# Third channel tile of a causal depthwise convolution moved from TensorE to ScalarE products and GpSimd sums

## The reference, cut to what matters

```python
h = val * sigmoid(gate)                                  # (1, 512 positions, 512 channels)
h = conv1d_depthwise_causal(h, cv_w, width=31) + cv_b    # out[c, s] = sum_n cv_w[n, c] * h[c, s - 30 + n] + cv_b[c]
h = silu(layer_norm(h, cv_ln_g, cv_ln_b))
```

## Time and profile before

| what | us |
|---|---|
| median of three executions | 2161.75 |
| the profiled execution's own time | 2158.83 |
| its span, first to last instruction | 2157.0 |
| `s5_and_conv`, start of its first to start of the next part's first work | 112.4 to 177.4 |
| mean granted PE clock, whole span | 0.976 of full |

### The profile page before, as it was taken

One profiled execution on the slowest core, in us unless ns is written; L12 is line 12 of the kernel. 1 busy time (PEld: TensorE's weight loads), 2 busy tenths in 40 slices (PEclk: granted clock), 3 DMA queues, 4 the chain that ended last, 5 costly groups with the idle time before them and its releaser, 6 DMA issues. The chain is left out here.

```text
span 2157.0 us, 26506 instructions
## 1 busy us (share of the span) xinstructions
PE 2008.3 (93%) x8626; PEld 1004.3 (47%) x8626; DVE 757.6 (35%) x2018; ACT 401.4 (19%) x880; POOL 263.5 (12%) x253
## 2 busy tenths in 40 slices
PE   8998989999999999977998888998999999999976
PEld 4553554444444444433457555554444444444432
DVE  4692352222222222234111778443222222222216
ACT  2103021111111111100001555211111111111110
POOL 0001100111111111100210000300111111111110
PEclk9999999999999999988998999999999999999998
DMA  7133156999999999879002000216899999999957
GB/s 228 8 62 144 66 220 245 396 417 405 410 397 405 405 395 391 345 293 271 0 0 79 1 1 2 94 49 253 317 407 399 417 408 407 398 413 401 402 222 324
DMA packets 107424, 566.06 MB, mean 262 GB/s; under 512 B 38624, under 2 KB 39392, under 8 KB 69088
## 3 DMA queue, kind: packets, MB, share of 16 engines
q1 hardware_dynamic: 79136, 498.06, 58.2%
q0 software_dynamic: 28224, 67.16, 7.9%
HBM read 539.84 MB, written 59.77 MB: 278 GB/s over the span
## 5 line engine op out<-in xcount | busy, mean ns | idle before, releaser
L438 PE MATMUL moe_bank<-moe_weights,moe_xgT 128*128 128x512 f32 x1024 | 457.0, 599 | 16.7 <-DMA moe_weights<-in_ex_weights 16.3
L438 PEld LDWEIGHTS moe_bank<-moe_weights,moe_xgT 128*128 128x128 f32 x1024 | 189.9, 190 | 233.5 <-issue 215.9
L746 DVE TENSOR_TENSOR moe_hid<-moe_sil,moe_bank 128x256 f32<-128x256 f32 x98 | 41.3, 422 | 659.1 <-ACT moe_sil L621 659.1
L471 PE MATMUL moe_bank<-moe_weights,moe_hidT 128*128 128x512 f32 x512 | 230.5, 593 | 0.0
L441 PE MATMUL moe_bank<-wide,moe_xgT 128*64 128x512 f32 x512 | 226.6, 595 | 0.0
L441 PE MATMUL moe_bank<-moe_weights,moe_xgT 128*64 128x512 f32 x512 | 226.6, 595 | 0.0
L314 POOL DMA_INDIRECT y<-moe_xy,moe_rows x98 | 98.9, 1009 | 945.7 <-DVE moe_idx L726 559.3
L621 ACT ACTIVATE moe_sil<-moe_bank 128x256 f32<-128x256 f32 x98 | 37.6, 383 | 658.6 <-PE moe_bank L438 457.2
L754 DVE TENSOR_SCALAR moe_xy<-moe_bank,moe_sgate 128x512 f32<-128x512 f32 x98 | 73.6, 751 | 219.5 <-PE moe_bank L471 142.1
L471 PEld LDWEIGHTS moe_bank<-moe_weights,moe_hidT 128*128 128x128 f32 x512 | 92.4, 191 | 93.4 <-issue 93.4
L299 POOL DMA_INDIRECT moe_xy<-h,moe_idx x98 | 100.2, 1022 | 267.9 <-DVE moe_idx L726 240.4
(11 more groups left out here) (354 smaller groups left out, 2416.3 us busy)
## 6 DMA issues: line engine op xcount, KB each, us to landing
moe_weights<-in_ex_weights SPq DMA_DIRECT2D x96, 2048.0 KB, 20.7
moe_weights<-in_ex_weights SPq DMA_DIRECT2D x96, 1024.0 KB, 17.9
wide<-in_ex_weights SPq DMA_DIRECT2D x34, 2048.0 KB, 22.4
wide<-in_ex_weights SPq DMA_DIRECT2D x34, 1024.0 KB
moe_weights<-y SPq DMA_DIRECT2D x18, 1024.0 KB, 20.6
wide<-y SPq DMA_DIRECT2D x8, 1024.0 KB, 7.8
moe_xy<-y SPq DMA_DIRECT2D x6, 1024.0 KB, 26.8
oddin_win<-in_od_w_in_heads SPq DMA_DIRECT2D x1, 4288.0 KB, 19.1
```

Of the source, the lines that this page charges most:

```text
L438: mm = pe.matmul(bG[:, :], xgT[:, n, :], wgu[j][:, :, n, :], start=(n == 0), stop=(n == KC - 1))
L471: mm = pe.matmul(bY[half][:, :], hidT[:, n, :], wdn[j][:, n, cols], start=(n == 0), stop=(n == HC - 1))
```

## The change

PLAIN becomes 2, so PAIRED becomes 2: PE keeps tiles 0 and 1, tile 3 stays on DVE as it was, and tile 2 becomes plain. ACT computes the 31 tap products of tile 2, the first two straight into the even and the odd sum, the other 29 into a ring of six buffers in `wide`. POOL adds product n into the sum of its parity, and at last the two sums into one. ACT's product n waits until POOL has made the sum that frees its buffer; POOL's sum n waits for the product and for the previous sum of the same parity. ACT issues products 0 to 18 ahead of its first copy, 19 to 24 between the copies of the two halves, and 25 to 30 after them. The shifted input of tile 2 is written by one DVE instruction instead of four, DVE makes no diagonals for it, and `wide` is filled to its last column (4096 + 2 x 512 + 6 x 512 = 8192).

```diff
-TAPS, CT, PLAIN = 31, 4, 1
+TAPS, CT, PLAIN, RING = 31, 4, 2, 6
 PAIRED = CT - PLAIN
...
-        odd_sums = wide_flat[:, PAIRED * 2 * NPAIR * HP:PAIRED * 2 * NPAIR * HP + PLAIN * SEQ].rearrange("p (t s) -> p t s", t=PLAIN)
+        spare = wide_flat[:, PAIRED * 2 * NPAIR * HP:].rearrange("p (t s) -> p t s", s=SEQ)
+        odd_sums, ring = spare[:, 0:PLAIN], spare[:, PLAIN:PLAIN + RING]
...
-        taps_v = s.sem("taps_dve")
+        taps_v, products_a, sums_p = s.sem("taps_dve"), s.sem("products_act"), s.sem("sums_pool")
...
             pool.memset(toep[:], 0.0).then_inc(cleared, 1)
             pool.memset(state[:, :, :, 0], 0.0).then_inc(padded, 1)
+            sums = [yT[:, CT + PAIRED, :], odd_sums[:, 0, :]]
+            for n in range(2, TAPS):
+                pool.wait_ge(products_a, n + 1)
+                if n >= 4:
+                    pool.wait_ge(sums_p, n - 3)
+                pool.tensor_tensor(sums[n % 2], sums[n % 2], ring[:, n % RING], ALU.add).then_inc(sums_p, 1)
+            pool.wait_ge(sums_p, TAPS - 2)
+            pool.tensor_tensor(sums[0], sums[0], sums[1], ALU.add).then_inc(sums_p, 1)
...
         def _(act):
+            def products(a, b):
+                for n in range(a, b):
+                    shifted, tap = e.h2[0][:, PAIRED, n:n + SEQ], plain_taps[:, 0, n:n + 1]
+                    if n == 0:
+                        act.activation(yT[:, CT + PAIRED, :], shifted, ACT.Identity, scale=tap, bias=col["cv_b"][:, PAIRED:PAIRED + 1]).then_inc(products_a, 1)
+                    elif n == 1:
+                        act.activation(odd_sums[:, 0, :], shifted, ACT.Copy, scale=tap).then_inc(products_a, 1)
+                    else:
+                        if n >= 2 + RING:
+                            act.wait_ge(sums_p, n - 1 - RING)
+                        act.activation(ring[:, n % RING], shifted, ACT.Copy, scale=tap).then_inc(products_a, 1)
+
+            products(0, 19)
             for b in range(4):
                 h, q = b // 2, b % 2
+                if b == 2:
+                    products(19, 25)
                 act.wait_ge(y_done, h + 1)
...
+            products(25, TAPS)
             for t in range(1, PAIRED):
                 act.wait_ge(conv_done, t + 1)
```

## The result

The changed kernel takes 2170.82 us (median of 8 runs, 2169.14 to 2171.64), the kernel before 2161.77 us in 8 runs beside them. The ratio is 1.0042, 95% interval [1.0029, 1.0055]: slower by 9 us, just under the 0.5% that the prediction had named as its bound. The prediction was 2172 us. The profiled execution took 2171.09 us, against a sum of 2170.4 made for such an execution; its span is 2169.3 us, 12.3 more than before.

A forecast was written before the change was run, and what follows sets the result against it. PE, with DVE close behind, bounds the part before the change; after it DVE would end last, at 187.2. 2158.8 + 10.6 for the part + 1.0 for the clock = 2170.4 us profiled, given as 2172; range 2147 to 2184.

The forecast's parts named there:

- PE and DVE relieved: Tile 2 off PE saves 13.85 us, its diagonals off DVE 2.3; PE would end at 162.0, DVE at 160.4.
- ACT: 31 products of 128x512 beside everything, 0.55 us apiece, costing nothing by their length.
- POOL's rate: 30 adds of 128x512 at 1.26 us, 37.8 us in all; POOL undisturbed would end at 154.4.
- The turns: POOL's adds and DVE's instructions alternate, 1.68 us per pair; DVE ends 26.8 us later, at 187.2.
- the lock: A two-SBUF-input DVE instruction and a POOL instruction reading SBUF exclude each other; the second waits for the first.
- (a): Rival, chance 0.18: wide instructions hardly block each other; the part ends with PE at 162.8, 2145 to 2148 us.
- the last seven adds: POOL's adds during DVE's plain sum, predicted to start at about 164 and end at about 176.
- (c): Rival, chance 0.15: DVE goes first wherever it queues without a gap, POOL last; +16.6 us and clock, 2177 to 2179.
- price per add: What each paid POOL add costs DVE: 1.03 us taken, bounded by nothing and 1.26 us.
- The clock: PE's slow clock at the next part's start, after some 9 us idle: between 0 and 2 us, 1 taken.
- The sum: Whole kernel: 2158.8 + 10.6 + 1.0 = 2170.4 us for the profiled execution; 2172 given.
- (b): Rival, chance 0.12: the engines share, an add costing DVE about 0.5 us; about 2157 us, no change told.

The follow-up runs named there:

- experiment 1: Changed kernel with POOL's 30 adds replaced by memsets of a 128x960 scratch tile, tile 2's sum left out; 2181.3 us, with one round of the experts more.
- experiment 5: Changed kernel with ACT issuing products 25 to 30 together with 19 to 24, ahead of the copies of half 1; 2169.27 us (1.0037).
- Experiment 2: Changed kernel with each multiply-add of DVE's plain sum waiting for the one just before it; 2169.82 us (1.0047).
- 3: Changed kernel with the 29 multiply-adds of DVE's plain sum made adds, tile 3's taps left out; 2163.15 us, one execution, other experts chosen.
- experiment 8: Changed kernel with POOL's adds gated as in experiment 6, but DVE's two sums of tile 3 left in SBUF; 2170.28 us (1.0052).
- experiment 6: Changed kernel with DVE's tile 3 sums in PSUM and POOL's adds kept out of the rotations, 26 after half 1's state; 2154.24 us (0.9972).

## Why the prediction was right

**PE and DVE relieved.** Right. Without collisions (experiment 1) the part ended with PE and ACT's copy, the next one starting at 164.49; the prediction had the copy end at 162.8 and 0.8 us to the next part, 163.6.

**ACT.** Right that its 31 products cost nothing, though each took 0.61 to 0.72 us and not 0.55. Product 18 and the copies behind it never waited for POOL in a way that mattered: the copies of half 0 came at 142.9, behind PE. It was POOL that waited: products 19 to 24 stand behind these copies, and POOL ran dry for 1.31 us, up to 145.25, while one of DVE's scans ran in its old 1.19 us.

**POOL's rate.** 1.26 us, as read from the odd mixer. Its first add took 1.58, behind DVE's copy of the decays.

**The turns.** The deciding step, and right for the rotations: 1.68 us for an add and a DVE instruction was predicted; POOL's adds there stand 1.67 to 1.68 us apart beside the multiplies and adds. The state of half 1 was ready at 156.1, predicted 156.9. Here the row seen with small instructions and the Trainium skill's rule ("SBUF — State Buffer", section "Who interferes with whom") gave the right answer for wide ones, which no row that the prediction shows had. The rule's half on writes bears out too: memsets left the two-operand instructions alone (0.68 us in experiment 1). They held up the copy, which the Trainium skill counts in the same section among the instructions that can take the shared ports.

One reading was missed. Against the lock the prediction counts that "no row shows a wide DVE instruction waiting". The trace of before has one, the copy of the decays behind the memset of `toep` (experiment 1). It is of another kind than the rotation's, but it takes away that point for (a).

**Where it failed.** The step "I take it that the two engines take turns when both have something queued" does not hold for the last seven adds: POOL had run out of products at 155.6, came back at 165.15 in the middle of DVE's unbroken chain and got in only at its end. DVE ended at 180.2 instead of 187.2 and POOL at 187.57 instead of 176: rival (c) for that stretch. It moved the sum little, since either way one of the two is always at work. In turns an add costs 1.02 us more, alone behind the chain 1.22, which for the last five adds makes about 1 us (an estimate); in experiment 5, with turns throughout, the part is 1.05 us shorter, counted from its first matmul. That the end came out at 187.57 on POOL for a predicted 187.2 on DVE is in this stretch luck: the price per add was right, the order was not. Experiment 2 shows that a gap opens the door, 3 that the kind of instruction doesn't matter, 5 and 8 that POOL keeps its turns in the same gapless chain if its adds run on into it. Why a fresh add stands in this chain and gets in between the diagonals (experiment 6) stays open.

**The clock.** The term of +1 us was near nothing in the next part. The windows view of the changed kernel:

```profile
148.00:156.00 8.00, 0.00 (x0) 0.00 (x0) 7.90 (x5) 0.23 (x1) 7.55 (x5) 0.50 0.30 85
156.00:168.00 12.00, 11.75 (x76) 8.41 (x78) 11.97 (x19) 4.62 (x8) 2.85 (x1) 0.50 0.13 23
...
182.00:192.00 10.00, 3.54 (x5) 1.58 (x6) 2.74 (x5) 3.57 (x4) 5.49 (x5) 0.51 0.23 69
```

After both idle times of PE, 9.68 and 8.92 us long, the granted clock was 0.50, that is 1.2 GHz: `across(1)` took 7.09 us instead of 3.79, tile 1's convolution 16.26 instead of 13.96, the mean 5.35 instead of 3.67. The first two hid behind POOL, the last behind the transfer for which the following matmuls wait: from the mean to the first matmul of the experts it is 28.79 us, before 28.80. So the term measured nothing. The prediction also had PE idle for about 12 us ahead of `across(1)`; it was 9.68, in part because tile 0's convolution took 15.65 us instead of 13.96, with a granted clock of 0.50 from 121 to 123 us behind an idle time of 3.12. In experiments 3 and 5 the same convolution took 13.96 behind the same idle time, so this differs from execution to execution.

**The sum.** +10.6 for the part was predicted, 11.05 measured. The median moved by 9.05 us, the profiled execution by 12.3; the part's own shift lies between them and within the interval of the ratio (6.3 to 11.9 us). That the sum of 2170.4 comes within 0.7 us of 2171.09 is more than it can claim: single executions of the kernel before range from 2155.85 to 2166.2. What it had right is the price of a turn.

**The rivals.** (a) needs what experiment 1 had to create, a POOL that reads nothing. (b) is out: an add cost 1.02 us, not 0.5. (c) held for the last seven adds only.

## What to carry to other kernels

GpSimd is no spare engine beside a VectorE that reads two operands from SBUF: here every 1.26 us add beside such instructions cost VectorE about 1 us, and beside its tensor_scalar from SBUF to SBUF as well (experiment 8). Before moving elementwise work there, list VectorE's instructions in that stretch by where their operands lie. If one operand can live in PSUM, or the GpSimd work can sit beside VectorE's PSUM reads, the overlap is real. With the sums in PSUM, the adds moved out of the rotations and five taps given back to VectorE, the change turned from 0.4% slower to 0.5% faster.

## What the runs showed of the hardware

- Who gets the next turn depends on how POOL comes to DVE's chain. An add that arrived fresh in the middle of a gapless one stood 14.54 us (12.78 in a chain of adds); adds that ran on into it got in after each DVE instruction, at 1.71. The rule is not complete: a fresh add got in between two gapless diagonals (2.30 us).
- DVE standing for POOL is counted as busy: 0.75 us instructions read 1.75, and the busy share of DVE rose while its work fell.
- In PSUM a multiply-add is as fast as in SBUF: 27 in 17.86 us, 0.66 for one.
- A 128x960 memset on POOL (0.9 us) leaves DVE's two-operand instructions alone but holds up a 128x1024 copy, which ended 0.54 us after the memset.
- A tensor_scalar of 128x512 from SBUF to SBUF, with one tensor to read, stands for POOL's adds as well (1.49 us for 0.54); into PSUM it doesn't (0.80 beside them, 0.81 without).
